# An opening by column quarters: modulation vectors made in four pieces beside the first matmuls of a transformer layer

## The reference, cut to what matters

```
ml = split(silu(c) @ ada_w + ada_b, 9)          # latent; c_ctx gives the same for the context
h  = rms_norm(x, ffn1_norm) * (1 + ml[1]) + ml[0]
x  = x + ml[2] * (0.5 * swiglu(h, w_gate, w_up, w_down))
lam_bar = exp(lam * dt); b_bar = ((lam_bar - 1) / lam) * b      # S5 set-up, wanted after the first segment
```

## Time and profile before

| | us |
|---|---|
| three runs | 1355.12, 1355.15, 1356.28 |
| median | 1355.15 |
| span of the profiled execution | 1354.2 |

### The profile page before, as it was taken

How to read it: one execution, slowest core, us unless ns; L and a number is a source line. 1 busy time by engine, 2 the same in 40 slices (tenths; PEclk the granted TensorE clock), 3 DMA queues, 4 the chain that set the end, 5 groups by cost and what they waited for, 6 DMA issues and landing times.

```text
span 1354.2 us, 21460 instructions
## 1 busy us (share of the span) xinstructions
PE 1333.5 (98%) x8546; PEld 1229.7 (91%) x8546; DVE 865.3 (64%) x1376; ACT 400.0 (30%) x757; POOL 651.0 (48%) x408
## 2 busy tenths in 40 slices
PE   5999999999999999999999999999999999999998
PEld 4899999999999999998888888888998999999997
DVE  5787368568556555437656649826778765555666
ACT  4320010210210110124635321222142555544455
POOL 1544444543543533532732356636467455655554
PEclk9999999999999999999999999999999999999999
DMA  9553354353444344223322479484736233344322
GB/s 357 161 148 85 121 148 120 120 157 116 126 135 139 102 126 158 62 55 109 80 62 52 126 212 259 152 266 148 229 87 199 63 94 94 107 115 114 101 72 85
DMA packets 236782, 178.18 MB, mean 132 GB/s; under 512 B 33416, under 2 KB 211852, under 8 KB 236684
## 3 DMA queue, kind: packets, MB, share of 16 engines
q1 hardware_dynamic: 216624, 145.78, 37.6%
q10 hardware_dynamic: 20060, 31.04, 7.0%
HBM read 156.93 MB, written 19.86 MB: 131 GB/s over the span
## 4 chain that ended last, share of the span: by engine, by line
PE 93%; DVE 3%; DMA 2%; SPq 1%; issue 1%; ACT 0%; DVEq 0%; ACTq 0%
PE ps L1244 47%; PE ps L1971 13%; PE ps L1566 13%; PE ps L2030 7%; DMA ada_w<-in_ada_w_dram 2%; PE ps L1255 1%; PE ps L1844 1%; DVE ada_acc L2860 1%; DVE ps L2972 1%; PE ps L2057 1%; PE ps L1881 1%; PE ps L1669 1%; PE ps L1487 1%; PE ps L1438 1%; PE ps L1706 1%
## 5 line engine op out<-in xcount | busy, mean ns | idle before, releaser
L1143 POOL TENSOR_SCALAR w_hi<-w_raw 128x1024 fp32r<-128x1024 f32 x128 | 153.4, 1198 | 527.8 <-PE ps L1244 276.0
L1146 POOL TENSOR_TENSOR w_lo<-w_raw,w_hi 128x1024 fp32r<-128x1024 f32 x128 | 325.4, 2542 | 10.7
L1244 PE MATMUL ps<-h_hi,w_lo 128*128 128x384 f32 (+2 forms) x1000 | 291.4, 351 | 0.0
L1244 PE MATMUL ps<-h_hi,w_hi 128*128 128x384 f32 (+2 forms) x1000 | 287.1, 346 | 0.0
L1244 PE MATMUL ps<-h_lo,w_hi 128*128 128x384 f32 (+2 forms) x1000 | 287.0, 346 | 0.0
L1244 PEld LDWEIGHTS ps<-h_hi,w_lo 128*128 128x128 f32 x1000 | 178.8, 188 | 14.9 <-issue 4.3
L1244 PEld LDWEIGHTS ps<-h_lo,w_hi 128*128 128x128 f32 x1000 | 180.6, 188 | 10.5
L1244 PEld LDWEIGHTS ps<-h_hi,w_hi 128*128 128x128 f32 x1000 | 180.4, 188 | 10.7
L1222 POOL TENSOR_TENSOR w_lo<-w_raw,w_hi 128x512 fp32r<-128x512 f32 x90 | 115.6, 1297 | 105.7 <-ACT w_hi L2609 104.2
L2860 DVE SCALAR_TENSOR_TENSOR ada_acc<-ada_w,cs,ada_acc 128x1024 f32<-128x1024 f32 x70 | 108.3, 1581 | 7.8 <-DMA ada_w<-in_ada_w_dram 5.5
L1971 PE MATMUL ps<-h_hi,w_hi 128*128 128x256 f32 x360 | 102.0, 283 | 0.0
(11 more groups left out here) (459 smaller groups left out, 2635.0 us busy)
## 6 DMA issues: line engine op xcount, KB each, us to landing
w_raw<-in_ffn_w_gate_dram SPq DMA_DIRECT2D x44, 512.0 KB, 5.1
w_raw<-in_ffn_w_up_dram SPq DMA_DIRECT2D x44, 512.0 KB, 4.1
w_raw<-in_ffn_w_down_dram SPq DMA_DIRECT2D x44, 512.0 KB, 4.5
ada_w<-in_ada_w_dram ACTq DMA_DIRECT2D x32, 512.0 KB, 3.9
w_raw<-in_w_in_dram SPq DMA_DIRECT2D x32, 512.0 KB, 4.3
ada_w<-in_ada_w_dram SPq DMA_DIRECT2D x30, 512.0 KB, 4.3
c_scr<-cp ACTq DMA_DIRECT2D x16, 288.0 KB, 3.8
b_scr<-bt_sb ACTq DMA_DIRECT2D x16, 256.0 KB, 3.9
```

Of the source, the lines that this page charges most:

```text
L1143: pool.tensor_scalar(w_hi[:, s, 0:cols], w_raw[:, s, 0:cols], 1.0, 1.0, ALU.mult, ALU.mult)\
L1146: pool.tensor_tensor(w_lo[:, s, 0:cols], w_raw[:, s, 0:cols], w_hi[:, s, 0:cols].bitcast(F32), ALU.subtract).then_inc(w_split, 1)
L1244: last = pe.matmul(mv[2], st, mv[part], start=(first and q == 0), stop=(n == len(terms) - 1 and q == 2))
```

## The change

Groups 1 and 0 are no longer taken one after the other and whole, but in four quarters of 256 columns, scale and shift of a quarter together. A quarter gives two k tiles of h. The order of loads is x, two weight units, quarter 0, the third weight unit, quarters 1 to 3; quarters 2 and 3 wait for row products that free their buffers. x is turned token tile by token tile as it lands. The square root is taken before silu. Three units instead of two are taken jointly, and the row products and turns of quarters 1 to 3 stand between their steps. POOL splits unit 2 after two tiles of `h_lo`. The S5 angles and roots are computed between the quarters, and `s5_powers` goes from behind pair 3 to in front of pair 0. `quarter_mod` on DVE adds the bias, makes the scale and applies both to two tiles; `quarter_low` makes their `h_lo`. `PLAIN` (tiles normalised ahead of the modulation) goes from 4 to 5. `keep_busy` is called in other places. The two row sums of a half (`ada_add` of group 2) and the wait in v = 7 are as they were.

```diff
 # SP
-            for k in range(KD):
-                sp.dma_start(first_tile(1, k), ada_src(1, k)).then_inc(ada_here0[1][k], 16)
-            sp.dma_start(raw(0, KD, P), first_src[0][:, :, 0:P]).then_inc(w_here[0], 16)
-            for k in range(KD):
-                sp.dma_start(first_tile(0, k), ada_src(0, k)).then_inc(ada_here0[0][k], 16)
-            sp.dma_start(raw(1, KD, P), first_src[1][:, :, 0:P]).then_inc(w_here[1], 16)
+            first_unit(0)
+            first_unit(1)
+            quarter(0)
+            first_unit(2)
+            quarter(1)
+            sp.wait_ge(row_made, 2)
+            quarter(2)
+            sp.wait_ge(row_made, 3)
+            quarter(3)
...
+                            if v == 3:
+                                sp.wait_ge(row_made, 4)
 # POOL
-                        if fresh and n < 4:
-                            is_done(pool, JOB["row1"])
-                            if n == 2:
-                                pool.wait_ge(h_ok, KD)
+                        if fresh and n == 2:
+                            pool.wait_ge(h_ok, 2)
 # PE
+            def row_products(q, g):
+                j = JOB["open"]
+                if q or not g:
+                    pe.wait_ge(row_ok, q + (q > 0 or g == 0))
+                pe.wait_ge(ada_here0[g][q], 16)
+                for k in range(KD):
+                    r = STRIP * (k % 4)
+                    last = pe.matmul(lat(j)[r:r + STRIP, QW * g:QW * g + QW], cs_wide[:, k, :], quarter_tile(g, q)[:, k, :],
+                                     start=(k < 4), stop=(k >= 4))
+                if g == 0 or q == 0:
+                    last.then_inc(row_made, 1)
+
+            def turn_rows(q, groups=(1, 0)):
+                j = JOB["open"]
+                pe.wait_ge(row_ok, q + 2 - (q == 0 and groups == (1,)))
+                for g in groups:
+                    for c in range(2):
+                        at = 8 * q + 4 * g + 2 * c
+                        last = pe.matmul(ctx_(j)[:, at:at + 2], ada_row[:, q % 2, QW * g + P * c:QW * g + P * c + P], strip_eye[:, 0:2],
+                                         start=True, stop=True)
...
+            for t in range(4):
+                turn_x(t)
+            turn_vecs()
+            for t in range(4, 6):
+                turn_x(t)
+            turn_lambda()
+            spread_roots()
...
+            keep_busy(8)
+            pe.wait_ge(cond_ok, 1)
+            row_products(0, 1)
+            keep_busy(3)
+            turn_rows(0, (1,))
+            keep_busy(6)
+            row_products(0, 0)
+            keep_busy(2)
+            pe.wait_ge(cond_ok, 3)
+            turn_rows(0, (0,))
+            keep_busy(8)
...
+                        joint_step((0, 1), 0)
+                        joint_step((0, 1), 1)
+                        row_products(1, 1)
+                        row_products(1, 0)
+                        joint_start(2)
+                        joint_step((2,), 0)
+                        turn_rows(1)
+                        joint_step((2,), 1)
+                        joint_step((0,), 2)
+                        row_products(2, 1)
+                        row_products(2, 0)
+                        joint_step((1,), 2)
+                        turn_rows(2)
+                        joint_step((2,), 2)
+                        joint_step((0, 1, 2), 3)
+                        row_products(3, 1)
+                        row_products(3, 0)
+                        joint_step((0,), 4)
+                        turn_rows(3)
+                        joint_step((1, 2), 4)
+                        joint_step((0, 1, 2), 5)
+                        joint_step((0, 1, 2), 6)
+                        joint_step((0, 1, 2), 7)
 # ACT
+            for q in range(QUARTERS):
+                for g in (1, 0) if q == 0 else (0,):
+                    act.wait_ge(row_made, q + 2 - g)
+                    if q >= 2:
+                        act.wait_ge(cols_made, q)
+                    c = slice(QW * g, QW * g + QW) if q == 0 else slice(0, 2 * QW)
+                    act.activation(ada_row[:, q % 2, c], lat(JOB["open"])[:, c], ACT.Copy).then_inc(row_ok, 1)
+                for k in (2 * q, 2 * q + 1):
+                    act.wait_ge(xn_ok, k + 1)
+                    act.activation(h_hi[:, k, :], scaled[:, k, :], ACT.Copy).then_inc(h_hi_ok, 1)
+                if q == 1:
+                    s5_trig()
 # DVE
+            for k in range(PLAIN):
+                plain_tile(k, j)
+            dve.wait_ge(cond_ok, 2)
+            quarter_mod(0)  
+            quarter_low(0)  
             for k in range(PLAIN, KD):
...
+            s5_angle()
+            quarter_mod(1)
+            quarter_low(1)
+            quarter_mod(2)
+            quarter_low(2)
+            s5_roots()
+            quarter_mod(3)
+            quarter_low(3)
+            dve.sem_inc(s5_in_used, 1)
             for k in range(2):
                 ada_add(ADA_START, k)
-            s5_angle()
+            s5_powers()
             ffn(JOB["ffn1"], PARTS1, NT, 0, 0)
...
-                            if f_ == 2:
-                                s5_roots()
-                            if f_ == 3:
-                                s5_powers()
```

More of the change, by code:

```diff
@@ L127 @@
 HT = NL // 2
-PLAIN = KD // 2
+PLAIN = 5
+QUARTERS = 4
+QW = D // QUARTERS
 HK = KD // 2
@@ L198, with x_job @@
 UNIT, JOB = {}, {}
+def x_job(t):
+    return JOB["x_first"] + t if t < 4 else JOB["x_rest"] + t - 4
 def _number(table, parts):
@@ L1269, in _, with turn_vecs @@
                 last.then_inc(job_done, 1)
[L1271 to L1285, removed]
+            def turn_vecs():
+                j = JOB["vec"]
+                wait_read(pe, j)
+                pe.wait_ge(vec_in, 16 * 9)
+                transpose(lat(j)[:, 0:P], vecs[:, :]).then_inc(job_done, 1)
@@ L1287, in keep_busy @@
             def keep_busy(n):
                 for _ in range(n):
[L1290 to L1296, removed]
-                    last = transpose(lat(j)[:, P * c:P * c + P], ada_row[:, g, P * c:P * c + P])
-                last.then_inc(job_done, jobs)
+                    pe.matmul(ctx_(JOB["ffn1"])[:, 0:P], ident[:, :], ident[:, :], start=True, stop=True)
@@ new lines, in turn_rows @@
+            def turn_rows(q, groups=(1, 0)):
[6 more added lines that the diff above has]
+                                         start=True, stop=True)
+                if q < QUARTERS - 1:
+                    last.then_inc(cols_made, 1)
+                else:
+                    last.then_inc(job_done, 1)
@@ L1479, in slot_free @@
                         pe.wait_ge(slot_read[j % 4], j // 4 + i * (part.jseg // 4))
-                    joint = 2 if two and part.segs + i == 0 else 0
+                    joint = JOINT if two and part.segs + i == 0 else 0
                     def joint_hi(v, k):
@@ L2123, in _, with row_squares @@
                 r0 += n
+            def row_squares(t):
+                act.wait_ge(x_here[t], 16)
+                act.activation(squares[:, t, :], x_in[:, t, :], ACT.Square, accum_out=root[:, t:t + 1]).then_inc(ms_ok, 1)
             for q, name in enumerate(("s5_lambda_re", "s5_lambda_im")):
@@ L2276, in ffn @@
                         seg(part, i)
-            act.wait_ge(xn_ok, KD)
-            act.wait_ge(shift_ok, 1)
-            for k in range(KD):
-                for c, v in ((slice(0, NL), 0), (slice(NL, NT), 1)):
-                    ins = act.activation(h_hi[:, k, c], scaled[:, k, c], ACT.Identity, bias=mod[:, k, v:v + 1])
-                ins.then_inc(h_hi_ok, 1)
             for g in range(4):
@@ L3371, in _, with quarter_low @@
+            def quarter_low(q):
+                for k in (2 * q, 2 * q + 1):
+                    dve.wait_ge(h_hi_ok, k + 1)
+                    TT(h_lo[:, k, :], scaled[:, k, :], h_hi[:, k, :].bitcast(F32), ALU.subtract).then_inc(h_ok, 1)
+            for t in range(6):
+                j = x_job(t)
                 is_done(dve, j)
-                dve.tensor_copy(x[:, k, :].rearrange("p (b c) -> p b c", b=2), both(j, 384)).then_inc(slot_read[j % 4], 1)
+                dve.tensor_copy(x[:, :, P * t:P * t + P], ps[:, 2 * (j % 4):2 * (j % 4) + 2, :].rearrange("p b (k c) -> p (b k) c", c=P))\
+                    .then_inc(slot_read[j % 4], 2 if t == 4 else 1)
@@ L3402, in _ @@
-            s5_lambda()
+            for t in (0, 3, 4, 5):
+                was_read(dve, x_job(t))
+            s5_lambda()
+            j = JOB["spread"]
+            is_done(dve, j)
+            for k in range(PLAIN):
+                plain_tile(k, j)
+            dve.wait_ge(cond_ok, 2)
+            quarter_mod(0)
+            quarter_low(0)
+            for k in range(PLAIN, KD):
+                last = plain_tile(k, j)
+            last.then_inc(slot_read[j % 4], 1)
+            s5_angle()
```

235 lines of the change are left out of this document (103 added, 132 removed).

## The result

The kernel after took 1367.38 us (median of four runs, 1365.19 to 1368.35), the kernel before beside it 1355.13. The ratio is 1.0085, with a 95% interval of 1.0070 to 1.0099: 0.85% slower. The forecast was 1359.3 with a range of 1352.0 to 1362.5, so the sign was right and the size was missed by 8 us. The profiled execution is the shortest of the four: 1365.19 for a span of 1363.5.

What follows compares the result with a forecast made beforehand. PE, busy 98%, bounds the kernel; the change counts by when v = 7's row sums start. Span 1354.2 + 2.9 (later sums) + 1.3 (low clock) = 1358.4; with the median 0.95 over the span, 1359.3 us, range 1352.0 to 1362.5.

Steps and rivals of the forecast that it cites:

- The opening up to the first joint step: PE's start through roots, spread, row products and first scaled tiles: first joint step at 28.2 us, before it was 40.94.
- The transfers: Loads of x, weight units and quarters in the opening: they land in time for PE and add nothing.
- The joint run: PE's three joint units: 35.7 us, ending at 63.9, or 64.7 with 0.8 for low clock, 2.2 earlier than before.
- The wait for quarter 1: PE in the joint run waits once for DVE's tile 2, ready at 39.4 against 37.4: 2.0 us, between 0 and 3.
- DVE's chain: DVE's work up to v = 7's accumulator: pair 0 starts at 77.8, accumulator done at 105.4, PE waiting since 100.4.
- The hindrance of `s5_powers` by POOL's splits: On DVE before pair 0: three POOL splits hold back the 21 operations, 6.0 us undisturbed; pair 0 at 77.8, bounds 69.7 to 80.5.
- The move as a block: DVE from pair 0's start to the finished accumulator: list unchanged, so it shifts whole and takes 27.6 us.
- the shift of the sums: PE in v = 7: the row sums start at 105.5 instead of 102.57, 2.9 us later.
- the clock behind the wait: After PE's 5.1 us wait in v = 7: 3.41 us at half clock, up to 1.7, taken as 1.3.
- The step from span to time: Whole kernel: the span is 0.95 us under the median of the runs, so 1358.4 becomes 1359.3.
- rival that DVE keeps up: Pair 0 starts by 72.8, no wait in v = 7, PE's list decides: 1352.6 us; chance 0.22.
- the opening itself loses: Clock falls before the roots and at quarter 1, joint run ends at 67 or later, DVE late: 1361 to 1362; chance 0.13.

Runs made afterwards that it cites:

- the two last experiments: Changed kernel, powers late, 8 more filling products: quarter 1's products earlier and angles later, 1353.53 us; then also its turn ahead of unit 2's two steps, 1352.57 us.
- The wait without the sums: Changed kernel with its wait in v = 7 kept and the 16 row sums left out, so the output lacks them: 1355.84 us.
- the delay in the kernel before: Kernel before, with 18 useless chained writes on DVE ahead of the first feed-forward pass, so the accumulator comes late: 1367.03 us, ratio 1.0087.
- the half filling: Changed kernel with 8 useless matmuls of 112 columns ahead of the wait in v = 7: 1366.86 us; with 16 it was 1358.39.
- the block of sums: Changed kernel, wait in v = 7 kept, the 16 row sums as one block behind v = 7's last product: 1363.24 us, ratio 1.0058.

## Why the prediction was wrong in size

**The opening up to the first joint step** (28.2): 29.5, the low clock included; that cost 1.7 (windows 17:20.4 and 20.4:23.8 at 0.59 and 0.90) where 0.8 was taken. Right within its bounds.

**The transfers** (no term): right. PE waited for none of quarters 1 to 3's loads; quarter 1's wait ended with ACT.

**The joint run** (64.7): 65.4 by the start of unit 3. The wait for quarter 1 was 1.34, not 2.0, and its cause was put incompletely: DVE's angles and the turn ended together, at 37.86, and with the angles out of the way the place of the turn in PE's list kept the wait at 1.27, as the two last experiments show. PE came to the wait in v = 7 at 101.3 instead of 100.4.

**DVE's chain** (pair 0 at 77.8, accumulator at 105.4): 78.42 and 104.44. The hindrance of `s5_powers` by POOL's splits was the best part of the forecast. The move as a block was 26.0 us instead of 27.6, mostly since its last two sums took 3.26 instead of 4.63, so PE's wait was 3.3 instead of 5.1 and the shift of the sums 2.0 instead of 2.9. The rule of exclusive access (the Trainium skill, SBUF — State Buffer, section Who interferes with whom) agrees with the trace: three DVE operations of 128 or 256 columns took 2.48 to 2.60 us, each until just after POOL's had ended. Of the two rows that the forecast read for this rule, the one at 60.86 is a TENSOR_SCALAR with one tensor input, so for two inputs it rests on the other one and on these three.

**The failed step** is the clock behind the wait: "a fall like that one, 3.41 us at half clock, costs up to 1.7, and I take 1.3". It cost 8.0. The size of the fall was taken from a place where row products and filling products followed it. The wait without the sums gives just that size: 3.4 us. But what stands behind this wait is v = 7 with a one-column sum between every two pairs, and that list, which ran at full clock in the kernel before, ran on at half clock here once the clock had fallen, in every profile in which it fell ahead of the sums or among the first of them (the kernel after, the delay in the kernel before, the half filling). With 8.0 and 2.0 in place of 1.3 and 2.9, the sum is 1354.2 + 10.0 = 1364.2 for the span, against 1363.5 measured. The median lies another 2.2 over the profiled execution. The step from span to time, 0.95, was too small as well: it was the distance of a median to the span of another execution, and in nearly all the runs that have both, the time is 1.7 to 1.8 over the span.

The Trainium skill (TensorE: Matmul & The Clock Gate, section HAM oscillation — how this bites in real kernels) tells of a clock lost anew at each of many waits. Here one wait was enough, with no idle time behind it, and the trace therefore goes beyond what that section describes.

The forecast's rival that DVE keeps up would have needed pair 0 by 72.8; with the powers out of the way it started at 66.66, and the time was 1354.9, not 1352.6, and its profile has two falls of the clock in the opening. They are what "the opening itself loses" was about. Taking the first away won 1.4 by the medians; the second, 3.3 us at half clock in that profile, is worth up to 1.6 in a run that has it. They did not decide.

Open is why the clock holds behind 3.4 us of waiting in one profile (the block of sums) and falls in another (no sums), with the same list up to there; and what made one run of eight long when the wait was filled. Open too is why the same list ran at full clock in the kernel before and did not come back from a low one: the runs show that it was so, not by what rule. And some runs are longer than their mean clock accounts for, as 1363.43 us at 0.997 with the delay.

## What to carry to other kernels

Price a wait of TensorE by what stands behind it: in two profiles, 3.3 to 3.4 us of idle time cost 1.7 us more when plain products followed and 8 more when one-column ones were mixed in. Before work is put in front of a deadline that an engine meets by 2.75 us, count that work with the interference of its neighbours (6.0 us became 14.6). Where a wait of TensorE can't be removed, filling it with products without use returned 9 of 12 us here, but half a filling returned 0.5.

## What the runs showed of the hardware

- Granted clock and busy share are different things: PE was marked busy for all of 17.0 us at 0.50.
- The same mixed list (a pair of wide products, then a row sum of one column) ran at 1.00 in the kernel before and at 0.50 in the kernel after, so what was granted depended on what had gone before. With 112 columns more per sum it was still 0.50.
- Sixteen row sums of one column (32 records of PE, 3.63 us) in a row, with no idle time ahead, were followed by 3.4 us at 0.55.
- The wait for quarter 1, 1.3 us, came with a fall in the profile with the powers late and with 1.00 in the profile of the kernel after; the list around it is the same. Idle stretches of 1.39 and 2.1 us in v = 7 were followed by a fall in their profiles; one of 3.4 us (the block of sums) was not.
- Twenty-one small operations of DVE took 6.0 us alone and 14.6 us beside three splits of POOL back to back; three of 128 or 256 columns took 2.48 to 2.60 us each.
